# The last two units in front of five norms finish token tile 0 first, with one weight part held back

## The chip, the cores and the metric

One core of a Trainium2 chip runs one program. The metric is the device time of an execution in microseconds, lower is better. The engines are PE (TensorE), ACT (ScalarE), DVE (VectorE), POOL (GpSimd) and SP (SyncE, which issues the loads). Each runs its own list of instructions in order, and they wait for each other through semaphores that are written out by hand.

## What is computed

Three transformer layers on 256 tokens of width 1024, all in float32. The parts around which the change lies, cut from the reference:

```python
def rms_norm_2(x, g):
    x32 = x.astype(jnp.float32)
    y = x32 * lax.rsqrt(jnp.mean(x32 * x32, axis=-1, keepdims=True) + EPS)
    return (y * g.astype(jnp.float32)).astype(x.dtype)

def ada_modulation(c, ada_w, ada_b):
    m = jax.nn.silu(c) @ ada_w + ada_b
    return jnp.split(m, N_MOD, axis=-1)

def even_layer(x, c, ...):
    sh_m, sc_m, g_m, sh_f, sc_f, g_f = ada_modulation(c, ada_w, ada_b)
    h = modulate(rms_norm_2(x, mix_norm), sh_m, sc_m)
    ...                                   # h @ w_in, convolutions, LRU
    x = x + g_m[:, None, :] * y           # y = ... @ w_out
    hf = modulate(rms_norm_2(x, ffn_norm), sh_f, sc_f)
    return x + g_f[:, None, :] * swiglu(hf, ffn_w_gate, ffn_w_up, ffn_w_down)
```

First comes a layer of attention and a squared-ReLU MLP with norms before and after each branch, then `even_layer`, then `odd_layer` (the same with attention in place of convolutions and LRU).

## The kernel before, in words

**Tokens.** The 256 tokens are two tiles of 128 partitions, tile 0 and tile 1. The residual `x` and the normed `xn` lie tokens by features. For the next product they are transposed by PE (`norm_T`, L1864: two groups of four 128x128 blocks for each tile) and copied out of PSUM as `aT_hi` (ACT, rounded, L753) and `aT_lo` (DVE, the rest, L1132).

**Weights.** All weights are streamed once. A unit is 2048 columns, two parts of 128x1024. A part is loaded into `w_raw`, rounded by ACT into `w_hi` (`split_part`, L700), and the rest is formed by DVE in `w_lo` (L1124). Each product is hi times hi, hi times lo and lo times hi. There are four slots, part v uses slot v modulo 4, and ACT's split of part v waits until PE has used part v-4 (`w_used`). The load of part v waits until DVE has formed the rest of part v-4.

**Norms.** Six places normalise `x`, numbered k = 0 to 5: before the first QKV, the MLP, w_in, the first SwiGLU, the second QKV and the second SwiGLU. Before each of k = 1 to 5 PE ends a projection into the four banks of `acc` (`acc[:, 2t+c]` is column half c of tile t). The last units are `out_unit` with `tile0=True` for k = 1, 3, 5 (the last unit runs tile 0 first, then signals `tile0_done`), and `down(..., final=True)` for k = 2 and 4. DVE adds the result to `x`, ACT squares and sums it, the reciprocal root comes from ACT or POOL, DVE scales (`norm_rows`, L1147), PE transposes, ACT and DVE copy, and `entry` starts the next product (L1909) with tile 0, transposing tile 1 in between.

**Order on ACT at k = 3, 4, 5** (`norm`): for t in 0, 1 it waits for `x_ready` of tile t and squares the whole row (L710). The copies `norm_hi(k, 0)` of tile 0's transposes stand behind both squares at k = 3 and 5, and between them at k = 4:

```python
for t in range(NT):
    act.wait_ge(x_ready, 2 * (k - 1) + t + 1)
    row_square(t, x[:, t, :])
    ...
    if t == 0 and k == 4:
        norm_hi(k, 0)
if k in (3, 5):
    norm_hi(k, 0)
```

**Modulation sums.** `mod` holds partial sums of the modulation over partitions. `ada_sums` multiplies it by a matrix of ones (L2089, float32, two instructions for a chunk of 512 columns), which sums over the partitions and spreads the result; ACT copies it back (`ada_parts`, L764). Three or four of these sums stand in front of the transposes of k = 1, 2, 3, 4, 5; at k = 1 and 2 a fourth stands in front of tile 1's transposes.

Of the kernel before, what the change touches and what calls it, by code (L numbers as in the profile page):

```python
# [32 lines left out]
P = 128  # L33
# [82 lines left out]
def block_program(nc, a, out):  # L116
    ctx = ExitStack()
    with ctx:
# [125 lines left out]
        def sum_bank(m):  # L244

            if m < 8:
                return (tp[:, 1, :] if m < 4 else acc[:, 1, :], ub[:, 0, :], ub[:, 1, :], acc[:, 2, :])[m % 4]
            return (tp if m < 12 else ub)[:, m % 2, :]

        def flat(h):  # L250
            return h.rearrange("p b n -> p (b n)")

# [36 lines left out]
        half_done = sem("half_done")  # L289
        tile0_done = sem("tile0_done")  # L290
        mix_loaded = [sem(f"mix_loaded{n}") for n in range(6)]
# [390 lines left out]
        def _(act):  # L682
# [13 lines left out]
            def split_part(v, i=None, per=0):  # L696
                act.wait_ge(w_loaded[v % SLOTS], plus(16 * (v // SLOTS + 1), i, 16 * 2 * per // SLOTS))
                if v >= SLOTS:
                    act.wait_ge(w_used, plus(v - SLOTS + 1, i, 2 * per))
                act.activation(w_hi[:, v % SLOTS, :], w_raw[:, v % SLOTS, :], ACT.Copy).then_inc(hi_done, 1)  # L700
# [143 lines left out]
            def mlp_norm(u):  # L844

                n_norm[0] += 1
                act.wait_ge(w_used, parts_to(u - 1))
                half_square(0, 0, acc[:, 0, :], sq_half)
                half_square(1, 0, acc[:, 2, :], sq_half)
# [3 lines left out]
                split_part(2 * u + 2)  # L853
# [8 lines left out]
                norm_hi(1, 0)  # L862
                split_part(2 * u + 3)
# [50 lines left out]
            def win_norm(u):  # L914
# [12 lines left out]
                split_part(2 * u + 2)  # L927
# [5 lines left out]
                norm_hi(2, 0)  # L933
                split_part(2 * u + 3)
# [172 lines left out]
        def _(dve):  # L1107
# [13 lines left out]
            def split_part(v, i=None, per=0):  # L1121
                dve.wait_ge(hi_done, hi_count(v, i, per))
                n = v % SLOTS
                dve.tensor_tensor(w_lo[:, n, :], w_raw[:, n, :], w_hi[:, n, :].bitcast(F32),  # L1124
# [15 lines left out]
            def norm_rows(t, g, shift):  # L1140
# [4 lines left out]
                for g in range(2):  # L1145
                    c = slice(g * CH, (g + 1) * CH)
# [581 lines left out]
            gated_norm_halves(4, U_SG1, GATE_M, G_F, SH_F, 22)  # L1728
# [6 lines left out]
        def _(pe):  # L1735
# [3 lines left out]
            def project_tile(v, t, k, outp, op_hi, op_lo, start, stop):  # L1739

                s, q = v % SLOTS, slice(t * P, (t + 1) * P)
                for n in range(2):
                    c = slice(n * CH, (n + 1) * CH)
                    pe.matmul(outp, op_hi[:, k + n, q], w_hi[:, s, c], start=start and n == 0, stop=False)  # L1744
                    pe.matmul(outp, op_hi[:, k + n, q], w_lo[:, s, c], start=False, stop=False)  # L1745
                    last = pe.matmul(outp, op_lo[:, k + n, q], w_hi[:, s, c], start=False, stop=stop and n == 1)  # L1746
                return last

            def project(u, h, bank, i=None, per=0, first=0, operand=None, tile0=False, lo_count=0, parts=(0, 1)):

                op_hi, op_lo = operand or (aT_hi[:, 4 * h:4 * h + 4, :], aT_lo[:, 4 * h:4 * h + 4, :])
                if lo_count:
                    for q in range(2):
                        part_ready(2 * u + q, i, per)
                        for t in range(NT):
                            for k in range(2 * q, 2 * q + 2):
                                c = slice((k % 2) * CH, (k % 2 + 1) * CH)  # L1760
                                for w in (w_hi, w_lo):
                                    pe.matmul(bank(t), op_hi[:, k, t * P:(t + 1) * P], w[:, (2 * u + q) % SLOTS, c],
                                              start=h == first and k == 0 and w is w_hi, stop=False)
                    pe.wait_ge(y_lo, lo_count)
                    for q in range(2):
                        for t in range(NT):
                            for k in range(2 * q, 2 * q + 2):
                                c = slice((k % 2) * CH, (k % 2 + 1) * CH)
                                last = pe.matmul(bank(t), op_lo[:, k, t * P:(t + 1) * P], w_hi[:, (2 * u + q) % SLOTS, c],
# [518 lines left out]
```

## Time and profile before

| | |
|---|---|
| three executions | 901.29, 901.52, 902.69 us, median 901.52 |
| profiled execution | 901.51 us, of which the span of instructions is 899.4 us |
| PE busy | 888.7 us, 99% of the span |
| DVE, ACT, POOL busy | 695.0, 487.3, 29.3 us |
| granted TensorE clock | 1.00 of full speed |

How to read it: time is microseconds from the first instruction. Matmuls are pipelined, so the time that a matmul adds is the distance from its start to the next one's, and a wait of PE is where this distance is longer than usual. "Idle before" in square brackets is shorter than such a wait, because the end of a matmul lies behind the start of the next one.

### The profile page before, as it was taken

Reading aid. Unit: us, or ns where it says so; the run is one execution under the profiler, and the core shown is the slowest. Engines: PE = TensorE matmul, PEld = TensorE weight load, DVE = VectorE, ACT = ScalarE, POOL = GpSimd, SP = SyncE. Lnnn points to the kernel's source line nnn. Section 1 sums busy time; section 2 is a strip of 40 time slices with the busy share of each in tenths; the row PEclk is TensorE's granted clock in tenths of the full one; section 3 lists DMA queues with packets and bytes.
Section 4 is the critical chain, followed back from the end, with each engine's and each line's share of the span. In section 5 each row is a group of like instructions: output and inputs, shape, how many; then the busy total and the mean of one; then the engine's idle time right before and its main releaser. Section 6 shows DMA issues by size and latency. Waiting matters only on the chain.

```text
span 899.4 us, 13652 instructions
## 1 busy us (share of the span) xinstructions
PE 888.7 (99%) x5057; PEld 761.6 (85%) x5057; DVE 695.0 (77%) x723; ACT 487.3 (54%) x651; POOL 29.3 (3%) x52
## 2 busy tenths in 40 slices
PE   8999999999999999999999999999999999999998
PEld 5998879999999699979888888878777888888886
DVE  5698978988888887996888888687796775655655
ACT  5545574444445758755455455455675465545542
POOL 4000100000000000011000000010000100000000
PEclk9999999999999999999999999999999999999999
DMA  6989586999898385556988887636434365555561
GB/s 217 341 276 340 175 293 208 365 358 320 333 326 316 102 277 170 181 165 201 360 304 318 318 297 280 189 98 211 137 115 142 117 209 190 187 187 186 187 188 69
DMA packets 117093, 208.08 MB, mean 231 GB/s; under 512 B 7236, under 2 KB 81068, under 8 KB 111928
## 3 DMA queue, kind: packets, MB, share of 16 engines
q1 hardware_dynamic: 116566, 205.31, 66.8%
q10 hardware_dynamic: 290, 2.10, 0.7%
q8 instruction: 30, 0.49, 0.2%
q14 instruction: 15, 0.12, 0.0%
q0 software_dynamic: 192, 0.05, 0.0%
HBM read 206.39 MB, written 1.05 MB: 231 GB/s over the span
## 4 chain that ended last, share of the span: by engine, by line
PE 94%; ACT 2%; DVE 2%; DMA 1%; issue 0%; SPq 0%; DVEq 0%; ACTq 0%
PE tp L1891 8%; PE ub L1891 8%; PE acc L1796 7%; PE acc L1797 7%; PE acc L1799 7%; PE acc L1744 5%; PE acc L1746 5%; PE acc L1745 5%; PE tp L1892 4%; PE ub L1892 4%; PE tp L1909 4%; PE acc L1909 4%; PE ub L1880 3%; PE ub L1879 3%; PE ub L1878 3%; PE acc L1878 3%
## 5 line engine op out<-in xcount | busy, mean ns | idle before, releaser
L1124 DVE TENSOR_TENSOR w_lo<-w_raw,w_hi 128x1024 fp32r<-128x1024 f32 x288 | 348.7, 1221 | 115.1 <-ACT w_hi L700 114.4
L700 ACT ACTIVATE w_hi<-w_raw 128x1024 fp32r<-128x1024 f32 x288 | 302.3, 1058 | 241.8 <-PE acc L1799 71.0
L1891 PE MATMUL tp<-aT,w_hi 128*128 128x512 f32 x320 | 114.1, 399 | 0.0
L1891 PE MATMUL ub<-aT,w_hi 128*128 128x512 f32 x320 | 113.8, 398 | 0.0
L1796 PE MATMUL acc<-w_hi,hT_hi 128*128 128x512 f32 x288 | 112.8, 392 | 0.1
L1797 PE MATMUL acc<-w_lo,hT_hi 128*128 128x512 f32 x288 | 112.2, 390 | 0.0
L1799 PE MATMUL acc<-w_hi,hT_lo 128*128 128x512 f32 x272 | 106.1, 390 | 0.0
L1892 PE MATMUL tp<-aT,w_lo 128*128 128x256 f32 x320 | 89.9, 281 | 0.0
L1892 PE MATMUL ub<-aT,w_lo 128*128 128x256 f32 x320 | 89.8, 281 | 0.0
L1891 PEld LDWEIGHTS tp<-aT,w_hi 128*128 128x128 f32 x320 | 60.1, 188 | 14.9
L1891 PEld LDWEIGHTS ub<-aT,w_hi 128*128 128x128 f32 x320 | 60.1, 188 | 14.6
L1878 PE MATMUL ub<-aT,w_hi 128*128 128x256 f32 x256 | 72.5, 283 | 0.0
L1880 PE MATMUL ub<-aT,w_lo 128*128 128x256 f32 x256 | 72.4, 283 | 0.0
L1879 PE MATMUL ub<-aT,w_hi 128*128 128x256 f32 x256 | 72.4, 283 | 0.0
L1744 PE MATMUL acc<-w_hi,aT 128*128 128x512 f32 x168 | 67.5, 402 | 0.2 <-DVE aT L1132 0.2
L1746 PE MATMUL acc<-w_hi,aT 128*128 128x512 f32 x168 | 65.5, 390 | 0.0
L1745 PE MATMUL acc<-w_lo,aT 128*128 128x512 f32 x168 | 65.5, 390 | 0.0
L1796 PEld LDWEIGHTS acc<-w_hi,hT_hi 128*128 128x128 f32 x288 | 54.1, 188 | 11.6 <-issue 0.3
L1797 PEld LDWEIGHTS acc<-w_lo,hT_hi 128*128 128x128 f32 x288 | 54.1, 188 | 10.5
L1892 PEld LDWEIGHTS ub<-aT,w_lo 128*128 128x128 f32 x320 | 60.4, 189 | 0.7
L1799 PEld LDWEIGHTS acc<-w_hi,hT_lo 128*128 128x128 f32 x272 | 51.1, 188 | 11.3
L1892 PEld LDWEIGHTS tp<-aT,w_lo 128*128 128x128 f32 x320 | 60.4, 189 | 0.0
(282 smaller groups left out, 1526.8 us busy)
## 6 DMA issues: line engine op xcount, KB each, us to landing
ada_raw<-in_l_ada_w SPq DMA_DIRECT2D x24, 1024.0 KB, 6.0
w_raw<-in_l_ffn_w_gate SPq DMA_DIRECT2D x44, 512.0 KB, 4.6
w_raw<-in_l_ffn_w_up SPq DMA_DIRECT2D x44, 512.0 KB, 3.8
w_raw<-in_l_ffn_w_down SPq DMA_DIRECT2D x44, 512.0 KB, 3.4
w_raw<-in_w_up SPq DMA_DIRECT2D x32, 512.0 KB, 4.5
w_raw<-in_w_down SPq DMA_DIRECT2D x32, 512.0 KB, 5.2
scratch<-in_l_ada_w SPq DMA_DIRECT2D x14, 1024.0 KB, 7.7
w_raw<-in_attn_w_qkv SPq DMA_DIRECT2D x24, 512.0 KB, 6.3
```

Source lines behind the costliest of these rows:

```text
L700: act.activation(w_hi[:, v % SLOTS, :], w_raw[:, v % SLOTS, :], ACT.Copy).then_inc(hi_done, 1)
L1124: dve.tensor_tensor(w_lo[:, n, :], w_raw[:, n, :], w_hi[:, n, :].bitcast(F32), ALU.subtract).then_inc(lo_done, 1)
L1744: pe.matmul(outp, op_hi[:, k + n, q], w_hi[:, s, c], start=start and n == 0, stop=False)
L1745: pe.matmul(outp, op_hi[:, k + n, q], w_lo[:, s, c], start=False, stop=False)
L1746: last = pe.matmul(outp, op_lo[:, k + n, q], w_hi[:, s, c], start=False, stop=stop and n == 1)
L1796: pe.matmul(outp, operand[0][:, k, q], w_hi[:, s, c], start=start, stop=False)
L1797: last = pe.matmul(outp, operand[0][:, k, q], w_lo[:, s, c], start=False, stop=False)
L1799: last = pe.matmul(outp, operand[1][:, k, q], w_hi[:, s, c], start=False, stop=stop)
L1878: pe.matmul(outp, wh, aT_hi[:, b, :], start=b == 0, stop=False)
L1879: pe.matmul(outp, wh, aT_lo[:, b, :], start=False, stop=False)
L1891: pe.matmul(banks[f], w_hi[:, v % SLOTS, c], aT[:, :, b, :], start=b == 0, stop=False)
L1892: last = pe.matmul(banks[f][:, 0:TOK], w_lo[:, v % SLOTS, c], aT_hi[:, b, :], start=False, stop=b == KB - 1)
```

## The change

The diff does five things.

- Before k = 1, 3 and 5 a new `out_last` takes the place of the last two units. With four parts v to v+3 it runs tile 0 with v, tile 1 with v, tile 0 with v+1 (signal `tile0_first`), tile 0 with v+2 and v+3 (signal `tile0_done`), and then tile 1 with v+1, v+2, v+3. Before k = 2 and 4 `down(..., left=...)` does the like: tile 1 with the second part of the last unit but one is run after `tile0_done`.
- Since part v+1 is held longer, a part four further on is put into a buffer that is idle then (`apart`), and the odd slots of the last layer change places (`slot_of`), so that the splits don't wait for the held part.
- Two sums stand before tile 0's transposes, the third directly behind them (`behind_T0`), the fourth before tile 1's transposes (`before_T1`), at all five places.
- DVE takes tile 0 whole first, then the first half of tile 1, then `norm_rows(0)`, and then the second half of tile 1. ACT's order is changed in `mlp_norm` and `win_norm` alone.
- `norm_rows` can wait for its shift by halves.

```diff
@@ ACT, mlp_norm
-                act.wait_ge(w_used, parts_to(u - 1))
+                act.wait_ge(tile0_first, 1)
                 half_square(0, 0, acc[:, 0, :], sq_half)
-                half_square(1, 0, acc[:, 2, :], sq_half)
                 act.wait_ge(tile0_done, 1)
                 half_square(0, 1, acc[:, 1, :], sq_done)
                 half_rstd(0, 1, 1)
-                split_part(2 * u + 2)
+                act.wait_ge(w_used, parts_to(u - 1))
+                half_square(1, 0, acc[:, 2, :], sq_half)
...
                 norm_hi(1, 0)
+                split_part(2 * u + 2)
                 split_part(2 * u + 3)
@@ ACT, win_norm
                 half_rstd(0, 1, 6)
-                split_part(2 * u + 2)
...
                 norm_hi(2, 0)
+                split_part(2 * u + 2)
                 split_part(2 * u + 3)
@@ DVE
             def gated_norm(n, u_end, g_mod, g, shift):
 
+                dve.wait_ge(half_done, n)
+                gated(0, g_mod, 0)
                 dve.wait_ge(tile0_done, n + 1)
-                gated(0, g_mod).then_inc(x_ready, 1)
+                gated(0, g_mod, 1).then_inc(x_ready, 1)
                 dve.wait_ge(x_ready, 2 * n + 1)
                 norm_scale(0, g)
+                dve.wait_ge(half_done, n + 1)
+                dve.tensor_tensor(xn[:, 1, 0:CH], acc[:, 2, :], g_mod[:, 0:CH], ALU.mult).then_inc(tile1_gated, 1)
+                norm_rows(0, g, shift)
                 dve.wait_ge(w_used, parts_to(u_end))
-                gate(1, g_mod)
-                norm_rows(0, g, shift)
+                gate(1, g_mod, 1)
+                dve.wait_ge(tile1_gated, 1)
                 add_gated(1).then_inc(x_ready, 1)
...
             def gated_norm_halves(n, u_end, g_mod, g, shift, out):
 
                 split_part(2 * u_end)
-                dve.wait_ge(w_used, parts_to(u_end - 1))
-                for t in range(NT):
-                    gated(t, g_mod, 0)
+                dve.wait_ge(tile0_first, n // 2 + 1)
+                gated(0, g_mod, 0)
+                if out:
+                    split_part(2 * u_end + 1)
                 dve.wait_ge(tile0_done, n + 1)
                 gated(0, g_mod, 1).then_inc(x_ready, 1)
                 dve.wait_ge(x_ready, 2 * n + 1)
                 norm_scale(0, g)
+                dve.wait_ge(w_used, parts_to(u_end - 1))
+                gated(1, g_mod, 0)
+                norm_rows(0, g, shift, out)
+                if not out:
+                    split_part(2 * u_end + 1)
                 dve.wait_ge(w_used, parts_to(u_end))
                 gated(1, g_mod, 1).then_inc(x_ready, 1)
-                if out:
-                    dve.wait_ge(ada_out, out)
-                norm_rows(0, g, shift)
-                split_part(2 * u_end + 1)
                 dve.wait_ge(x_ready, 2 * n + 2)
                 norm_scale(1, g)
@@ PE, entry
                 norm_T(k, 0)
+                behind_T0()
...
@@ PE, new
+            def out_last(u, order, lo_count=0):
+                v, h = 2 * u + 4, order[2][1]
...
+                else:
+                    part_ready(v)
+                    tile(0, 0)
+                    tile(1, 0).then_inc(w_used, 1)
+                    part_ready(v + 1)
+                    tile(0, 1).then_inc(tile0_first, 1)
+                for p in (2, 3):
+                    part_ready(v + p)
+                    last = tile(0, p)
+                last.then_inc(tile0_done, 1)
+                for p in (1, 2, 3):
+                    tile(1, p).then_inc(w_used, 1)
@@ PE, down, final
                     lo(0, 1, 1).then_inc(tile0_done, 1)
+                    if left:
+                        for n in range(2):
+                            last = down_block(2 * u - 1, left[0], 1, n, False, False, operand=operand)
+                        last.then_inc(w_used, 1)
@@ PE, before the entries
-            ada_sums(0, 0, 3)
-            entry(U_MLP, tp_banks, before_T1=lambda: ada_sums(0, 3, 4), tile1_out=1)
+            ada_sums(0, 0, 2)
+            entry(U_MLP, tp_banks, lambda: ada_sums(0, 2, 3), lambda: ada_sums(0, 3, 4), tile1_out=1)
...
-            ada_sums(1, 0, 4)
             def swiglu(layer):
...
-                entry(u, tp_banks, gated=True)
+                m = 8 * layer
+                ada_sums(1, m, m + 2)
+                entry(u, tp_banks, lambda: ada_sums(1, m + 2, m + 3), lambda: ada_sums(1, m + 3, m + 4), gated=True)
```

## Rows read from the trace of the kernel before

**Rows 1.** The page, part 1: busy us, share of the span, instructions.
```profile
PE 888.7 (99%) x5057; PEld 761.6 (85%) x5057; DVE 695.0 (77%) x723; ACT 487.3 (54%) x651; POOL 29.3 (3%) x52
```

**Rows 2.** Waits of PE: waiting line, releaser: us in total, times, longest.
```profile
PE acc L1909 <- ACT aT L753: 1.7, 3, 0.9
```

**Rows 3.** Timeline of PE at k = 3: start us, us, instruction, count.
```profile
389.07 0.39 PE L1744 MATMUL acc<-w_hi,aT 128*128 128x512 f32 x1
...
394.51 3.98 PE L2089 MATMUL ub<-ada_raw,ones 128*128 128x512 f32 x8
...
399.62 0.74 PE L1909 MATMUL tp<-w_hi,aT 128*128 128x256 f32 x4
...
403.71 1.03 PE L1864 MATMUL acc<-ident,xn 128*128 128x128 f32 x8
```

**Rows 4.** Timeline of DVE at k = 3.
```profile
389.58 1.23 DVE L1124 TENSOR_TENSOR w_lo<-w_raw,w_hi 128x1024 fp32r<-128x1024 f32 x1 [1.10 <-ACT w_hi L700]
390.73 0.68 DVE L1243 TENSOR_TENSOR xn<-acc,mod 128x512 f32<-128x512 f32 x1
...
392.05 0.68 DVE L1243 TENSOR_TENSOR xn<-acc,mod 128x512 f32<-128x512 f32 x1
...
396.81 0.69 DVE L1247 TENSOR_TENSOR x<-x,xn 128x512 f32<-128x512 f32 x1
397.42 1.41 DVE L1147 SCALAR_TENSOR_TENSOR xn<-xn,rstd,mod 128x512 f32<-128x512 f32 x2
```

**Rows 5.** Timeline of ACT at k = 3.
```profile
388.42 2.01 ACT L700 ACTIVATE w_hi<-w_raw 128x1024 fp32r<-128x1024 f32 x2 [3.47 <-PE acc L1769]
...
397.53 1.06 ACT L710 ACTIVATE scratch<-x 128x1024 f32<-128x1024 f32 x1 [0.50 <-DVE x L1247]
...
398.97 1.20 ACT L753 ACTIVATE aT<-acc 128x512 fp32r<-128x512 f32 x2 [0.28 <-PE acc L1864]
```

**Rows 6.** Timeline of PE at k = 5.
```profile
704.14 3.70 PE L2089 MATMUL ub<-mod,ones 128*128 128x512 f32 x8
...
708.96 0.74 PE L1909 MATMUL tp<-w_hi,aT 128*128 128x256 f32 x4
...
713.00 1.04 PE L1864 MATMUL acc<-ident,xn 128*128 128x128 f32 x8
```

**Rows 7.** Timeline of ACT at k = 5: the copy of the second sum.
```profile
706.06 0.60 ACT L764 ACTIVATE mod<-ub 128x512 f32<-128x512 f32 x1 [0.26 <-PE ub L2089]
```

**Rows 8.** Timeline of PE at k = 2.
```profile
302.38 1.02 PE L2089 MATMUL acc<-mod,ones 128*128 128x512 f32 x2
...
305.31 1.32 PE L1864 MATMUL tp<-ident,xn 128*128 128x128 f32 x8 [0.20 <-DVE xn L1147]
307.57 1.19 PE L1909 MATMUL acc<-w_hi,aT 128*128 128x512 f32 x4 [0.94 <-ACT aT L753]
```

**Rows 9.** Timeline of DVE at k = 2.
```profile
298.29 1.23 DVE L1124 TENSOR_TENSOR w_lo<-w_raw,w_hi 128x1024 fp32r<-128x1024 f32 x1 [0.36 <-ACT w_hi L700]
...
304.52 1.40 DVE L1147 SCALAR_TENSOR_TENSOR xn<-xn,rstd,mod 128x512 f32<-128x512 f32 x2
```

**Rows 10.** Timeline of PE at k = 4.
```profile
586.03 1.88 PE L2089 MATMUL ub<-mod,ones 128*128 128x512 f32 x4
...
591.83 1.18 PE L1909 MATMUL acc<-w_hi,aT 128*128 128x512 f32 x4 [0.25 <-ACT aT L753]
...
595.86 1.03 PE L1864 MATMUL ub<-ident,xn 128*128 128x128 f32 x8
```

**Rows 11.** Timeline of DVE at k = 4.
```profile
586.09 1.23 DVE L1138 TENSOR_TENSOR xn<-x,mod 128x1024 f32<-128x1024 f32 x1
...
588.61 1.41 DVE L1147 SCALAR_TENSOR_TENSOR xn<-xn,rstd,mod 128x512 f32<-128x512 f32 x2
```

**Rows 12.** Timeline of PE at k = 1.
```profile
120.41 1.18 PE L1909 MATMUL tp<-w_hi,aT 128*128 128x512 f32 x4
```

**Rows 13.** Timeline of PE at k = 0, the first products of the program.
```profile
9.24 2.07 PE L1909 MATMUL acc<-w_hi,aT 128*128 128x512 f32 x4 [0.49 <-ACT aT L753]
```

More of the change, by code:

```diff
@@ L1760, in project @@
                                 c = slice((k % 2) * CH, (k % 2 + 1) * CH)
-                                for w in (w_hi, w_lo):
-                                    pe.matmul(bank(t), op_hi[:, k, t * P:(t + 1) * P], w[:, (2 * u + q) % SLOTS, c],
-                                              start=h == first and k == 0 and w is w_hi, stop=False)
+                                for w in (rounded_part, rest_part):
+                                    pe.matmul(bank(t), op_hi[:, k, t * P:(t + 1) * P], w(2 * u + q)[:, c],
+                                              start=h == first and k == 0 and w is rounded_part, stop=False)
                     pe.wait_ge(y_lo, lo_count)
@@ L1847, in down @@
                                 last = pe.matmul(acc[:, 2 * t + n, :], hT_lo[:, 2 * h, t * P:(t + 1) * P],
-                                                 w_hi[:, v % SLOTS, n * CH:(n + 1) * CH], start=False, stop=False)
+                                                 rounded_part(v)[:, n * CH:(n + 1) * CH], start=False, stop=False)
                     else:
-                        for t in range(NT):
+                        for t in range(1 if left and k == 1 else NT):
                             for n in range(2):
                                 last = down_block(v, 2 * h + k, t, n, first and k == 0, False, operand=operand)
-                    last.then_inc(w_used, 1)
+                    if not (left and k == 1):
+                        last.then_inc(w_used, 1)
             n_norm = [0]
@@ L1908, in products @@
                         width = HALF if gated else CH
-                        last = pe.matmul(out, op[:, b, t * P:(t + 1) * P], w[:, v % SLOTS, n * width:(n + 1) * width],
+                        last = pe.matmul(out, op[:, b, t * P:(t + 1) * P], part[:, n * width:(n + 1) * width],
                                          start=begin and n == 0, stop=end and n == blocks - 1)
@@ L1924, in entry @@
                         half(t, p)
-                        if t == 0 and w is w_hi:
+                        if t == 0 and w is hi:
                             pe.wait_ge(hi_done, hi_count(2 * u + p))
@@ L1928, in entry @@
                             part_ready(2 * u + p)
-                        products(t, p, aT_hi, w, p == 0 and w is w_hi)
+                        products(t, p, aT_hi, w, p == 0 and w is hi)
                     if t == 0:
@@ L1942, in entry @@
                         for p in range(2):
-                            products(1, p, aT_lo, w_hi).then_inc(w_used, 1)
+                            products(1, p, aT_lo, rounded_part).then_inc(w_used, 1)
                     else:
@@ L1950, in entry, with no_sums @@
                     part_ready(2 * u + p)
-                    products(0, p, aT_hi, w_lo, end=p == 3)
-                    products(1, p, aT_hi, w_lo)
-                    products(1, p, aT_lo, w_hi, end=p == 3).then_inc(w_used, 1)
+                    products(0, p, aT_hi, rest_part, end=p == 3)
+                    products(1, p, aT_hi, rest_part)
+                    products(1, p, aT_lo, rounded_part, end=p == 3).then_inc(w_used, 1)
+            def no_sums():
+                return None
             def hidden_T(h, out):
@@ L2085, in ada_sums @@
                     c, m = ADA_ORDER[layer][n], 12 * layer + n
-                    if m >= 8:
+                    if m >= 8 and m not in (18, 19):
                         pe.wait_ge(ada_out, m - 1)
@@ L2184, in one @@
                     pe.wait_ge(hT_lo_done, plus(j0 + j, i, 2))
-                    down(v + 2, (j - 1) % 2, i, 6, first=j == 1)
+                    down(v + 2, (j - 1) % 2, i, 6, first=j == 1, left=last_left if i is None and j == NJ_SG - 1 else ())
                 one(1)
```

160 lines of the change are left out of this document (102 added, 58 removed).

## Prediction

> **What bounds the kernel now.** The page first: PE is busy 99% of the span [rows 1], so the time is PE's work plus its waits, and the change adds or removes no matmul, load or copy. What it can win or lose is PE's waits at five places. The waits of PE come next: the products behind the norms wait 1.7 us for ACT's copies of the transposes, three times [rows 2]. Then the timeline around each norm, where the distance from one start to the next is set against the usual one. The usual ones: 24 matmuls from 389.07 to 394.51 are 0.2267 each [rows 3]; a sum is two instructions of 0.43, so 0.86 (four take 1.88, of which the last's own length is 0.60) [rows 10]; eight transposes are 8 x 0.109 = 0.87; a product of the SwiGLU entry (256 columns) is 0.12. By these, PE loses about 0.8 us at k = 1, 1.9 at k = 2, 1.1 at k = 3, 1.9 at k = 4 and 0.7 at k = 5: 6.4 us in all are there to be won.
>
> The method for each place is the same. The first sum begins where the units end, and that doesn't move, since the units keep their matmuls. From there I put down PE's own list (two sums, transposes, sum, products, sum, transposes of tile 1) and see whether what it needs from ACT and DVE is later. The result is how far the transposes of tile 1 move, because behind them nothing waits before or after. A release comes 0.4 us after the start of the last matmul of a group, since one lasts 0.39 [rows 3].
>
> **k = 2 (w_in): gain 1.35.** Tile 0 is done 6 matmuls, 1.36 us, sooner. ACT's split of the second w_in part doesn't wait for the held part, so DVE's rest of it starts behind the instruction before at 297.85 and not at 298.29, where it stood 0.36 for ACT [rows 9]; the scaling of tile 0's second half, which waited for tile 0's end, follows at 299.6 and not 300.6. All behind it shifts by 1.0: `norm_rows(0)` from 304.52 to 303.5 [rows 9]. PE ends two sums at 302.38 + 1.72 = 304.1 [rows 8] and transposes at 304.3, not 305.31 [rows 8]. ACT's split of 1.06 that stood in front of tile 1's squares goes behind the copies, so these come at 305.0. The third sum covers them: 304.3 + 0.2 + 0.87 + 0.86 gives the first product at 306.3, not 307.57 [rows 8]. With the 0.1 that a product costs behind a wait, the gain is 1.35. The moved splits end at 308.1, and PE asks for the later one at 306.3 + 10 x 0.2267 = 308.5: cover of 0.4.
>
> **k = 4 (second QKV): gain 1.6.** Counted back from the first sum at 586.03 [rows 10], tile 0's first half is released 25 matmuls before it, at 586.03 - 5.67 + 0.4 = 580.8, and all of tile 0 at 586.03 - 19 x 0.2267 + 0.4 = 582.1. ACT's second split doesn't wait for the held part and ends at 580.1, DVE's rest behind it at 581.6. Two halves of 1.32 [rows 4] end at 584.2; before, tile 0 was whole just ahead of 586.09, and `norm_rows(0)`, at 588.61, began 2.5 behind it [rows 11]. Of these 2.5, 2.1 are the square and POOL's root and the rest is a gate of tile 1 that stood in the way; so it begins at 586.5 at the latest, if the root is alone. PE has ended two sums at 586.03 + 1.72 = 587.75 [rows 10], transposes at once, and sums until 589.5; ACT's copies begin at 588.4 and hide behind the third. First product 589.5 and not 591.83 [rows 10]: 2.3 sooner, of which 0.86 is the fourth sum, only moved; 0.1 is won at the first product. Tile 1's transposes then come at 594.2, not 595.86 [rows 10].
>
> **k = 1 (MLP): gain 0.1.** `norm_rows(0)` comes 0.7 sooner, but PE stood only 0.1 us for it. Two sums, the transposes and the third sum end at 120.36, and the first product began at 120.41 before [rows 12]; the list is the same and only a stand of 0.1 goes. For tile 1 ACT now has two splits (1.06 + 0.96) between the copies and the squares and not one, which eats the 0.7: tile 1 is normed between 0.1 sooner and 0.2 later. I take 0.1 sooner.
>
> **k = 3 (first SwiGLU): loss 1.8.** Here the order on ACT is unchanged: the copies of tile 0's transposes stand behind the square of tile 1's row, which waits for `x_ready` of tile 1. The change puts `norm_rows(0)` and a split of DVE in front of that `x_ready`. DVE's list: ACT's split is released 4 matmuls sooner (388.42 less 0.91) [rows 5], so DVE's rest begins at 388.6 and gives place after 1.15 [rows 4]. Two halves of tile 0 at 1.32 each (390.73 to 392.05) end at 392.5; `norm_scale` takes 1.26 (its 1.23 and the wait for its own end) [rows 11]; a half of tile 1 1.32; `norm_rows` 1.33 (1.41, but each instruction gives place 0.08 before its end, as 389.58 to 390.73 shows for one of 1.23); the split 1.14; the last half of tile 1 1.41, to its end [rows 4]. That ends at 399.0. Before it was 396.81 + 0.69 = 397.50 [rows 4]. ACT squares from 399.0, gives place after 1.04, copies for 0.6 (two take 1.20) [rows 5]: first product 400.7, not 399.62 [rows 3]. PE has done two sums, transposes and the third sum by 394.51 + 1.72 + 0.87 + 0.86 = 398.0 and stands for 2.7 us. From the first product to tile 1's transposes it was 4.09 (399.62 to 403.71) [rows 3], of which 0.2 were small waits that go; the fourth sum comes in: 400.7 + 3.9 + 0.86 = 405.5, which is 1.8 later than 403.71.
>
> **k = 5 (second SwiGLU): loss 2.3.** The same order. DVE is early, but `norm_rows(0)` of the second half waits for the second sum's copy, which starts at 706.06 and takes 0.60 [rows 7], and PE's sums don't come sooner. So it runs 706.7 to 707.4, the last half of tile 1 ends 1.41 later at 708.8, the square gives place at 709.85, and the first product comes at 710.5, not 708.96 [rows 6]. PE's third sum ends at 708.8: a stand of 1.7 us, beside 0.85 and 0.4 before the two groups of transposes. Then 3.9 + 0.86: tile 1's transposes at 715.3 and not 713.00 [rows 6].
>
> **Sum.** -0.1 - 1.35 + 1.8 - 1.6 + 2.3 = +1.05 us. The buffers `apart` cost nothing: they are written by the same split, and the loads of the parts concerned have landed before. What the trace doesn't show is a change of weights from transposes to a sum and on to a product without a wait between: between 0 and 0.1 us at each of five places; I take 0, by the matmul behind another kind, and 0.5 for the range. Against the profiled execution, 901.51, which is the median, this gives 902.6.
>
> **A clock that falls.** The first products of the program take 2.07 for four [rows 13], where four take 1.18 at k = 1 [rows 12]: a start distance of 0.43 and not 0.23, PE's lower of two levels, though the page's granted clock says 1.00. After that no matmul of the trace is so slow, and the longest stand is 1.1 us, at k = 2 (305.31 + 0.87 + 0.3 of waits within, to 307.57) [rows 8]. The change makes one of 2.7. The Trainium skill ("TensorE: Matmul & The Clock Gate", What's actually happening) says that the array falls to half its rate after a stretch of idleness and comes back after a stretch of work; the trace agrees at the program's start, and no row shows it for a stand of 2 to 3 us.
>
> **Rivals.**
> - *The two SwiGLU norms don't stall (faster).* If the copies of tile 0 don't end up behind the later square, or DVE's list is 2 us shorter than my sum, k = 3 gives -1.1 and k = 5 +0.5 (its `norm_rows` still waits for the sum's copy). Then it is -0.1 - 1.35 - 1.1 - 1.6 + 0.5 = -3.6: 897.9. For it: DVE's work at k = 3 does begin 1 us sooner. Against it: the order on ACT as it stands in the code. If only one of the two stalls goes, 899.7 to 900.
> - *The clock falls in a stand (slower).* It decides at the stand of 2.7 us at k = 3, or at those of k = 5. At the start PE is slow from 6.8 to 12.4; as much at half the rate costs 2.8 us. One fall gives 905.4, two 908.
> - *The change doesn't do what it says*: `tile0_first` or the held part brings nothing at k = 2 and 4, because another wait (a load, a split) ends last. Then it is +4.0: 905.5. Against it: the loads for these parts have landed more than 1 us before.
>
> **How the numbers follow.** The forecast 902.6 has a chance of 0.68 and its own range 901.7 to 903.8 (0.3 for each DVE list, 0.5 for the changes of weights). The faster rival with its in-between cases has 0.17, the clock 0.09, no gain at k = 2 and 4 0.06. For 8 in 10 the range is 898.8 to 904.8. A measurement can tell about 0.2%, 1.8 us, from no change. Above 903.3 lie the two slower rivals and a fifth of the forecast, 0.28; below 899.7 most of the faster rival, 0.15; between them 0.57.
>
> **What would show it.** Right: at k = 3 a wait of L1909 for ACT's aT of over 2 us with the square of tile 1 (L710) just before the copy; at k = 5 one of some 1.6; at k = 2 the product at 306.3 and at k = 4 at 589.5; start distances of 0.227 behind the stands. Wrong: the copy (L753) at k = 3 in front of the second square, `x_ready` of tile 1 before 398, distances of 0.43 behind a stand, or waits of PE for `w_hi` or `w_lo` inside the entries.

## The result, and the profile after

The changed kernel takes 904.29 us (median of 9 executions, 902.78 to 906.05), the kernel before 901.59 us (9 executions, 901.29 to 902.69). The ratio is 1.0025, with a 95% interval of 1.0017 to 1.0034. The forecast of 902.6 and its range (898.8 to 904.8) hold that median, but the direction doesn't agree with the likeliest case: 2.7 us more is slower by over 0.2%, which had a chance of 0.28. The range holds it by 0.5 us, and the same kernel's second median below (904.81) lies on its edge.

The nine executions are of two kinds. In four (902.78, 902.97, 903.02, 903.23) TensorE's mean granted clock is 0.999 or 1.0, and their mean is 903.0. In five (904.29, 904.63, 905.10, 905.23, 906.05) it is 0.998, and their mean is 905.1. The profiled one is 903.23, of the first kind, with a span of 901.1. The page has PE busy 99% of it, as in [rows 1]. A stand is a stretch in which PE does nothing and waits. Its length is given here as the profile counts idle time, which is 0.16 us less than the distance of starts makes it at k = 3 and 5. The waits of PE (engine, tile and line, what was waited for: us in total, times, the longest), against [rows 2]:

```profile
PE tp L1934 <- ACT aT L779: 4.1, 2, 2.6
PE acc L2052 <- DMA gain<-in_norm_mix_pre: 2.7, 1, 2.7
PE acc L1888 <- DVE xn L1175: 0.7, 1, 0.7
```

In the new line numbers L1934 are the products, L1888 the transposes, L2158 the sums, L779 ACT's copies of the transposes, L736 the square of a row, L1175 the normed rows. The two waits that make 4.1 us are new: they stand in front of the first products of the two SwiGLU norms, k = 3 and k = 5. The first wait of the program (gain) is 2.7 where the trace of before has 2.3, and in the traces below between 2.3 and 3.1: it lies ahead of all that was changed, and it moves everything behind it. So 0.4 of the 1.7 us between the two profiled executions is no effect of the change.

The timeline of PE at k = 3 (start, duration, engine, line, operation, tiles, count, idle time before and what ended it), which answers to [rows 3]:

```profile
393.58 1.88 PE L2158 MATMUL ub<-ada_raw,ones 128*128 128x512 f32 x4
395.30 1.07 PE L1888 MATMUL acc<-ident,xn 128*128 128x128 f32 x8
396.21 1.02 PE L2158 MATMUL ub<-ada_raw,ones 128*128 128x512 f32 x2
399.84 0.74 PE L1934 MATMUL tp<-w_hi,aT 128*128 128x256 f32 x4 [2.61 <-ACT aT L779]
...
401.86 2.11 PE L1934 MATMUL tp<-w_hi,aT 128*128 128x256 f32 x16
403.81 1.02 PE L2158 MATMUL ub<-ada_raw,ones 128*128 128x512 f32 x2
404.67 1.04 PE L1888 MATMUL acc<-ident,xn 128*128 128x128 f32 x8
405.46 0.72 PE L1934 MATMUL tp<-w_hi,aT 128*128 128x256 f32 x4
```

The transposes follow the first two sums at once, 1.72 us behind the start of the first one where it was 3.82 before, and with the third sum done PE stands 2.6 us. The same stretch of DVE and of ACT shows why:

```profile
394.25 1.41 DVE L1175 SCALAR_TENSOR_TENSOR xn<-xn,rstd,mod 128x512 f32<-128x512 f32 x2
395.57 1.22 DVE L1150 TENSOR_TENSOR w_lo<-w_raw,w_hi 128x1024 fp32r<-128x1024 f32 x1
...
397.43 0.69 DVE L1275 TENSOR_TENSOR x<-x,xn 128x512 f32<-128x512 f32 x1
```

```profile
398.16 1.06 ACT L736 ACTIVATE scratch<-x 128x1024 f32<-128x1024 f32 x1 [2.06 <-DVE x L1275]
...
399.21 1.07 ACT L779 ACTIVATE aT<-acc 128x512 fp32r<-128x512 f32 x2
```

ACT is idle for 2.06 us with the finished transposes in front of it: its next instruction in order is the square of tile 1's row, which waits for DVE's last sum of `x`, and the copies (L779) stand behind it. At k = 5 it is the same picture, [rows 6] before and this after:

```profile
703.53 1.88 PE L2158 MATMUL ub<-mod,ones 128*128 128x512 f32 x4
706.10 1.44 PE L1888 MATMUL acc<-ident,xn 128*128 128x128 f32 x8 [0.69 <-DVE xn L1175]
...
709.88 0.74 PE L1934 MATMUL tp<-w_hi,aT 128*128 128x256 f32 x4 [1.48 <-ACT aT L779]
...
714.71 1.04 PE L1888 MATMUL acc<-ident,xn 128*128 128x128 f32 x8
```

At k = 2 and k = 4 the stands are gone ([rows 8] and [rows 10] before):

```profile
304.62 1.32 PE L1888 MATMUL tp<-ident,xn 128*128 128x128 f32 x8
...
306.24 1.49 PE L1934 MATMUL acc<-w_hi,aT 128*128 128x512 f32 x4
...
312.24 0.93 PE L1934 MATMUL acc<-w_hi,aT 128*128 128x512 f32 x3
```

```profile
588.71 1.04 PE L1888 MATMUL tp<-ident,xn 128*128 128x128 f32 x8
...
590.05 1.47 PE L1934 MATMUL acc<-w_hi,aT 128*128 128x512 f32 x4
...
596.03 1.17 PE L1934 MATMUL acc<-w_hi,aT 128*128 128x512 f32 x4
```

**The account.** One mark for each place, the start of the first product behind the transposes of tile 1, gives what each did. In the trace of before these are the lines

```profile
126.01 1.17 PE L1909 MATMUL tp<-w_hi,aT 128*128 128x512 f32 x4
...
313.16 1.17 PE L1909 MATMUL acc<-w_hi,aT 128*128 128x512 f32 x4
...
404.50 1.67 PE L1909 MATMUL tp<-w_hi,aT 128*128 128x256 f32 x12
...
596.65 1.17 PE L1909 MATMUL acc<-w_hi,aT 128*128 128x512 f32 x4
...
713.79 1.67 PE L1909 MATMUL tp<-w_hi,aT 128*128 128x256 f32 x12
```

and in that of after, beside the last lines of the views above at k = 2, 3 and 4,

```profile
126.32 0.93 PE L1934 MATMUL tp<-w_hi,aT 128*128 128x512 f32 x3
...
715.50 0.72 PE L1934 MATMUL tp<-w_hi,aT 128*128 128x256 f32 x4
```

Before and after: 126.01 and 126.32 at k = 1, 313.16 and 312.24 at k = 2, 404.50 and 405.46 at k = 3, 596.65 and 596.03 at k = 4, 713.79 and 715.50 at k = 5. The lead or lag (after less before) goes +0.31, -0.92, +0.96, -0.62, +1.71, and the steps of it, with the 0.43 of the program's start (the first sum of k = 1 comes at 116.85 and not 116.42) taken from the first, are -0.12, -1.23, +1.88, -1.58, +2.33. Their sum is +1.28, and 0.43 + 1.28 = 1.71 is the difference of the two profiled executions (1.72). What is left of the 2.7 us of the medians is not in this trace: it is in the executions that show the lower mean clock.

### The profile page after: what moved, and what is told of

The parts are those of the page before. It is cut to its first block, busy times and chain, and to the rows that moved or that the text cites. A ratio compares the mean times of both kernels' runs of the same rounds, so it can differ in the third digit from the quotient of the medians.

```text
span 901.1 us, 13655 instructions
## 1 busy us (share of the span) xinstructions
PE 887.9 (99%) x5057; PEld 761.9 (85%) x5057; DVE 694.9 (77%) x726; ACT 487.3 (54%) x651; POOL 28.9 (3%) x52
## 3 DMA queue, kind: packets, MB, share of 16 engines
HBM read 206.39 MB, written 1.05 MB: 230 GB/s over the span
## 4 chain that ended last, share of the span: by engine, by line
PE 95%; DVE 3%; ACT 1%; DMA 1%; issue 1%; SPq 0%; ACTq 0%; DVEq 0%
PE tp L1915 8%; PE ub L1915 8%; PE acc L1816 7%; PE acc L1817 7%; PE acc L1819 7%; PE acc L1779 5%; PE acc L1781 5%; PE acc L1780 5%; PE tp L1916 4%; PE ub L1916 4%; PE acc L1934 4%; PE tp L1934 4%; PE ub L1904 3%; PE ub L1903 3%; PE ub L1902 3%; PE acc L1902 3%
## 5 line engine op out<-in xcount | busy, mean ns | idle before, releaser
L1150 DVE TENSOR_TENSOR w_lo<-w_raw,w_hi 128x1024 fp32r<-128x1024 f32 x283 | 342.6, 1222 | 110.4 <-ACT w_hi L726 110.0
L726 ACT ACTIVATE w_hi<-w_raw 128x1024 fp32r<-128x1024 f32 x283 | 296.6, 1058 | 232.8 <-PE acc L1819 67.4
L1779 PE MATMUL acc<-w_hi,aT 128*128 128x512 f32 x160 | 64.4, 402 | 0.2 <-DVE aT L1158 0.2
L1781 PE MATMUL acc<-w_hi,aT 128*128 128x512 f32 x160 | 62.4, 390 | 0.0
L1780 PE MATMUL acc<-w_lo,aT 128*128 128x512 f32 x160 | 62.4, 390 | 0.0
```

The lines of the kernel that those rows point to most:

```text
L726: act.activation(rounded_part(v), w_raw[:, v % SLOTS, :], ACT.Copy).then_inc(hi_done, 1)
L1150: dve.tensor_tensor(rest_part(v), w_raw[:, v % SLOTS, :], rounded_part(v).bitcast(F32), ALU.subtract).then_inc(lo_done, 1)
L1779: pe.matmul(outp, op_hi[:, k + n, q], wh[:, c], start=start and n == 0, stop=False)
L1780: pe.matmul(outp, op_hi[:, k + n, q], wl[:, c], start=False, stop=False)
L1781: last = pe.matmul(outp, op_lo[:, k + n, q], wh[:, c], start=False, stop=stop and n == 1)
```

## The experiments

The theory behind all of them: PE's time goes by its own ordered list and by the two ordered lists of ACT and DVE. The loss at k = 3 and 5 is made by ACT's order (copies behind a square that waits for a later `x`), the gain at k = 2 and 4 is real, and the rest of the slowdown is TensorE's clock falling behind the stand at k = 3. The kernel before was timed beside each group: 901.49 for the first four, 901.58 for the next four, 902.09 for the last two, on another chip each time.

**1. The changed kernel once more.** No edit.

> The changed kernel itself, unaltered, as the measure for the others. Its nine executions so far lie in two groups: four of 902.8 to 903.2 us with a granted clock of 0.999 to 1.000, five of 904.3 to 906.1 with 0.998. Theory A (the stands of PE at k = 3 and k = 5 sometimes let the clock fall): again two groups, about half of the executions 1.3 to 3 us above the lowest and with the lower clock. Rival B (the spread was that chip's or that hour's): one group within 0.5 us near 903.

904.81 us (903.03 to 905.38, 7 executions), ratio 1.0031 [1.0020, 1.0042]. One execution has a clock of 1.0 (903.03), six have 0.997 or 0.998 (904.33 to 905.38, mean 904.8). Here the profiled execution is of the second kind (904.87), so the fall can be seen. The timeline of PE at k = 3:

```profile
400.03 0.75 PE L1934 MATMUL tp<-w_hi,aT 128*128 128x256 f32 x4 [2.61 <-ACT aT L779]
400.62 0.99 PE L1934 MATMUL tp<-w_lo,aT 128*128 128x256 f32 x4
401.40 1.05 PE L1934 MATMUL tp<-w_hi,aT 128*128 128x256 f32 x4
402.26 1.05 PE L1934 MATMUL tp<-w_lo,aT 128*128 128x256 f32 x4
403.11 2.50 PE L1934 MATMUL tp<-w_hi,aT 128*128 128x256 f32 x16
```

Between the starts of groups of four lie 0.78, 0.86 and 0.85 us, so 0.213 for each product of the last two groups, where the trace above has 0.12 (16 products from 401.86 to 403.81). The table of stretches gives the granted clock for it (stretch, its length, busy time and count of PE, PEld, DVE, ACT, POOL, then the clock, the DMA share and GB/s):

```profile
400.00:405.00 5.00, 4.97 (x29) 4.97 (x30) 3.75 (x5) 2.84 (x4) 2.37 (x3) 0.66 0.05 16
405.00:420.00 15.00, 15.00 (x109) 13.81 (x108) 7.83 (x8) 7.37 (x9) 2.76 (x3) 1.00 0.49 146
```

The clock is 0.66 in the 5 us behind the stand and 1.00 in the other stretches of the table: for about 3.6 us PE runs at its lower level, 1.2 GHz. Some 17 products at 0.094 us more each cost 1.6 us. Behind the stand of k = 5, which is 1.5 us, nothing of the kind is seen (1.00 from 710 to 716).

**2. Both copies first.** In ACT's norm, at k = 3 and 5, the copies of tile 0 and the splits of the next weights go in front of the square of tile 1; nothing else of the change is touched.

```diff
-                    if t == 0 and k == 4:
+                    if t == 0 and k in (4, 3, 5):
                         norm_hi(k, 0)
+                        if k != 4:
+                            split_hi(u + 1)
                 if k in (3, 5):
-                    norm_hi(k, 0)
-                if k in (3, 5):
-                    split_hi(u + 1)
                     ada_parts(layer, parts[2], parts[3])
```

> The changed kernel, but at k = 3 and 5 ACT copies tile 0's transposes and makes the two splits before it squares tile 1's row. Theory (the square of tile 1 in front of the copies is what makes PE stand): the stand of 2.77 at k = 3 and that of 1.64 before the first product at k = 5 go; tile 1's transposes come 2.3 sooner at k = 3 (then limited by tile 1's norm) and 1.5 at k = 5; span 897.2, time 899.3, 0.25% under the kernel before. Rival (the copies wait for something else, such as tile 0's norm or PE): no more than 0.5 us changes. On the clock: by theory A all executions show 1.000 and lie within 0.5 us; by rival B the spread stays.

898.93 us (898.57 to 899.29, 6), ratio 0.9969 [0.9957, 0.9981], no execution with a lower clock: 4.1 us less than the changed kernel's executions whose clock holds, and 5.4 less than its median. The timeline of PE and of ACT at k = 3:

```profile
396.25 1.02 PE L2157 MATMUL ub<-ada_raw,ones 128*128 128x512 f32 x2
396.71 1.04 PE L1933 MATMUL tp<-w_hi,aT 128*128 128x256 f32 x4
```

```profile
396.04 1.08 ACT L778 ACTIVATE aT<-acc 128x512 fp32r<-128x512 f32 x2
...
398.89 1.07 ACT L736 ACTIVATE scratch<-x 128x1024 f32<-128x1024 f32 x1
```

The copies start at 396.04 and not 399.21, the products at 396.71 and not 399.84, right behind the sum. (The product is recorded 0.46 us behind the start of a sum that takes 0.86, so the distance of 3.1 us says too much: tile 1's transposes come at 402.23 and not 404.67, 2.4 us sooner.) The square of tile 1 comes 0.7 later than it did, and PE doesn't ask for it. So the copies' place in ACT's list is what makes the stand.

**3 and 4. One of the two places alone.** The same edit at k = 3 only, and at k = 5 only (`k in (4, 3)`, `k in (4, 5)`).

> The same order of ACT at k = 3 alone, so the stand of 1.64 at k = 5 (and 0.85 before the transposes there) stays. Theory: span 898.8, time 900.9. Clock: if only a stand as long as the 2.77 at k = 3 lets it fall, none falls here; if the 1.64 at k = 5 is enough, some executions lie 1.3 to 3 us higher with 0.998.

> The same order of ACT at k = 5 alone, so the stand of 2.77 at k = 3 stays. Theory: span 899.6, time 901.6 in the executions whose clock holds. Clock: if the stand at k = 3 is the cause, about half of the executions fall to 0.998 and lie 1.3 to 3 us higher; if it is the one at k = 5, none.

At k = 3 alone: 900.79 us (900.09 to 901.58, 11), ratio 0.9989 [0.9980, 0.9998], no lower clock in 11 executions, although the stand of k = 5 is still there. At k = 5 alone: 902.86 us (901.18 to 903.58, 11), ratio 1.0011 [1.0002, 1.0020]; eight of 11 show a clock of 0.997 or 0.998 (mean 903.1), three hold it (901.18, 901.33, 901.83, mean 901.4). In its trace the stretch behind the stand of k = 3 has again a clock of 0.66:

```profile
400.00:405.00 5.00, 4.84 (x28) 4.84 (x29) 3.75 (x5) 2.97 (x5) 2.37 (x3) 0.66 0.07 23
```

Against the 903.0 of the changed kernel with its clock held, mending k = 3 gives 2.2, mending k = 5 gives 1.6, and both give 4.1. The lower clock belongs to the stand at k = 3 and goes with it.

**5. The kernel before with a stand made by hand.** Does the stand itself lower the clock, or something else that the change brought? The kernel before gets three squares more on ACT at k = 3, in front of its copies, chained one behind the other (two of a whole row, one of half a row; nobody reads them).

```diff
+                if k == 3:
+                    act.wait_ge(sq_done, n_sq[0])
+                    for width in 2 * (D,) + 1 * (CH,):
+                        chained(act.activation(squares[:, 1, 0:width], x[:, 1, 0:width], ACT.Square))
                 if k in (3, 5):
                     norm_hi(k, 0)
```

> The kernel before, with nothing of the change, but at k = 3 ACT squares tile 1's row again, twice whole and once by half, each waiting for the one ahead, in front of the copies of tile 0's transposes (nobody reads these squares; the output is unaffected). PE then stands about 3.0 us behind the transposes where it stood 0.3. Theory (a stand of this length is by itself enough to let the clock fall): 904.1 in the executions whose clock holds, and in half of them or more a clock of 0.998 and 1.6 more, 905.7. Rival (the fall needs something else of the change, such as the four sums and their order before the stand, or is this program's loads): all executions at 904.1 with 1.000.

904.98 us (903.88 to 906.20, 6), ratio 1.0036 [1.0024, 1.0049]. Three executions hold the clock (903.88, 903.94, 904.66), three don't (905.30, 905.34, 906.20). The kernel before, timed beside it, has no lower clock in 17. The trace is of one that holds it:

```profile
402.86 0.74 PE L1913 MATMUL tp<-w_hi,aT 128*128 128x256 f32 x4 [2.67 <-ACT aT L757]
403.44 0.64 PE L1913 MATMUL tp<-w_lo,aT 128*128 128x256 f32 x4
```

So the stand alone, in a kernel without any of the change, is enough, and the fall isn't certain. That the length differs from one execution to the next doesn't explain it: the two traces of the changed kernel both have a stand of 2.61 at k = 3, and the clock holds in the first and falls in the second. A fall costs 1.5 us here (means 904.2 and 905.6).

**6. A shorter stand.** In the changed kernel, at k = 3 alone, the fourth sum comes directly behind the third, so PE has 0.86 us more work before the stand, which is 1.75 us then and not 2.61. All else, ACT's order too, is as changed.

```diff
-                entry(u, tp_banks, lambda: ada_sums(1, m + 2, m + 3), lambda: ada_sums(1, m + 3, m + 4), gated=True)
+                if layer:
+                    entry(u, tp_banks, lambda: ada_sums(1, m + 2, m + 3), lambda: ada_sums(1, m + 3, m + 4), gated=True)
+                else:
+                    entry(u, tp_banks, lambda: ada_sums(1, m + 2, m + 4), no_sums, gated=True)
```

> The changed kernel with one sum moved: at k = 3 the fourth sum stands behind the third, behind tile 0's transposes, and no longer before tile 1's. It fills 0.86 of the stand, which falls from 2.77 to 1.9; the copies don't come sooner. Theory (the loss at k = 3 is the stand of 1.0 beyond before plus the sum that was moved behind it): 0.86 less than the changed kernel where the clock holds, 902.2. Rival (PE's place is set by tile 1's norm and not by its own list): no gain. On the clock: 1.6 let none of eleven executions fall, 2.77 let nine of eleven; if the length decides, few or none fall at 1.9 and the median is 902.3, 2.5 under the changed kernel's.

902.08 us (901.66 to 903.71, 11), ratio 1.0008 [0.9999, 1.0017], no lower clock in 11 executions.

```profile
395.91 1.88 PE L2158 MATMUL ub<-ada_raw,ones 128*128 128x512 f32 x4
399.55 0.75 PE L1934 MATMUL tp<-w_hi,aT 128*128 128x256 f32 x4 [1.75 <-ACT aT L779]
```

(The expectation counts stands by distance, 2.77 and 1.9, and its nine falls of eleven are eight in the record of `copies_first_k5`.) The sum is now hidden in the stand, which is worth its 0.86, and the fall is gone: 903.0 - 0.9 = 902.1. This separates the two parts of the loss.

**7. Only k = 2 and 4.** The change with k = 1, 3 and 5 put back to what they were before (units, order of ACT and DVE, sums). The two places with `down(..., left=...)`, for which the gain was forecast, stay. Of the edit, the two cuts on PE that take back the units and the sums at k = 5 and at k = 3 and 5:

```diff
-                    if n < 28:
-                        out_unit(U_WOUT1, OUT_LO_FIRST, n // 2 - 12, (hT_hi, hT_lo), parts=(n % 2,))
-                    elif n == 28:
-                        out_last(U_WOUT1, OUT_LO_FIRST)
+                    if n != 31:
+                        out_unit(U_WOUT1, OUT_LO_FIRST, n // 2 - 12, (hT_hi, hT_lo) if n < 28 else None,
+                                 parts=(n % 2,))
...
-                ada_sums(1, m, m + 2)
-                entry(u, tp_banks, lambda: ada_sums(1, m + 2, m + 3), lambda: ada_sums(1, m + 3, m + 4), gated=True)
+                ada_sums(1, m, m + 4)
+                entry(u, tp_banks, no_sums, no_sums, gated=True)
```

> The change at k = 2 and 4 alone: held part, order of ACT and DVE and places of the sums there; k = 1, 3 and 5 as in the kernel before. Theory (the places are independent and each is worth what its stretch of the trace shows, 1.23 and 1.58 us): 901.5 - 2.8 = 898.7. Rival (a gain at one place is given back at the next, since splits, loads or tile 1's chain fall behind): more than 900.

898.83 us (898.51 to 899.53, 6), ratio 0.9968 [0.9955, 0.9980]: 2.75 us less than before, where the account above has 1.23 + 1.58 = 2.81. The rival that nothing is gained at k = 2 and 4 falls. It is also as fast as `copies_first`: with ACT's order mended, the new scheme at k = 3 and 5 brings nothing on balance. By the same marks as above, `copies_first` gains 0.6 at k = 3 and loses 0.8 at k = 5, where the transposes wait for the rows that are normed from the second sum's copy.

**8. The sums of k = 5 sooner.** `copies_first`, and at k = 5 the first two sums between the end of tile 0 and tile 1's parts, so that their copies are there in time; ACT's splits on either side of its square.

```diff
-def out_last(u, order, lo_count=0):
+def out_last(u, order, lo_count=0, between=None):
...
                 last.then_inc(tile0_done, 1)
+                if between:
+                    between()
...
-                        out_last(U_WOUT1, OUT_LO_FIRST)
+                        out_last(U_WOUT1, OUT_LO_FIRST, between=lambda: ada_sums(1, 8, 10))
```

> The kernel with the copies in front of the square at k = 3 and 5, and at k = 5 also the first two sums between the end of tile 0 and tile 1's parts in the last units, with one split behind the square. Theory (at k = 5 tile 0's norm waits for the copy of the second sum, which starts 1.9 us behind the end of the units): the 0.85 and 0.30 in front of the two groups of transposes go, tile 1's transposes then wait for their own norm, in all 1.0 less: 897.9. Rival (DVE's additions to x are what ends last there): no gain, 898.9.

898.26 us (898.17 to 899.61, 5), ratio 0.9966 [0.9952, 0.9979], where 897.9 was expected. The two waits in front of the groups of transposes at k = 5 went, and a new one came in the products, for the second split:

```profile
707.48 1.66 PE L1937 MATMUL tp<-w_hi,aT 128*128 128x256 f32 x12 [0.47 <-ACT w_hi L726]
```

**9. The same with both splits in front of the square.** 

```diff
                         if k == 5:
-                            split_part(2 * u + 2)
-                if k == 5:
-                    split_part(2 * u + 3)
+                            split_hi(u + 1)
```

> sums_early with one line moved: at k = 5 both splits of ACT stand in front of the square of tile 1, and not one on either side. In sums_early the second split was waited for by PE (0.63 us at 706.7), while the normed tile 1 was ready 1.6 us before PE asked for it, so the square may come 1.0 us later. Theory (PE's own list with the waits of ACT and DVE on it): the 0.63 goes, about 0.1 of it turns up elsewhere, 898.26 - 0.55 = 897.7, and no execution with a lower clock. Rival (tile 1's norm is what ends last at k = 5): the transposes of tile 1 wait for the later square and it stays at 898.3 or rises to 898.7.

898.16 us (897.47 to 898.73, 5) beside 902.09 for the kernel before on that chip, ratio 0.9952 [0.9939, 0.9966]. The wait for the split is gone, and the transposes of tile 1 begin without one and take 0.2 us longer (1.01 us from their start to the next product, 0.79 in `sums_early`):

```profile
706.88 2.08 PE L1935 MATMUL tp<-w_hi,aT 128*128 128x256 f32 x16
708.80 1.02 PE L2161 MATMUL ub<-mod,ones 128*128 128x512 f32 x2
709.66 1.26 PE L1889 MATMUL acc<-ident,xn 128*128 128x128 f32 x8
```

So the rival (tile 1's norm ends last) isn't what the trace shows, beyond those 0.2. The time alone doesn't decide it: 898.16 as measured lies beside the rival's 898.3, while on 901.5 the ratio is 897.2, near the 897.7 expected. Its interval and that of `sums_early` overlap, so what lies between the two is seen in the traces and not in the times. Of all kernels here this one stands lowest against the kernel before.

**10. DVE's order put back.** The loss has two halves in the code: ACT's copies stand behind the square, and DVE now norms tile 0 ahead of the last half of tile 1, which makes the square late. Experiment 2 takes away the first. This one takes away the second and leaves ACT as it is.

```diff
                 gated(1, g_mod, 0)
-                norm_rows(0, g, shift, out)
                 if not out:
                     split_part(2 * u_end + 1)
                 dve.wait_ge(w_used, parts_to(u_end))
                 gated(1, g_mod, 1).then_inc(x_ready, 1)
+                norm_rows(0, g, shift, out)
```

> The changed kernel, with only DVE's order of before restored at k = 3 and 5: the last half of tile 1's gate and sum stands in front of the normed rows of tile 0, and ACT's order stays. x_ready of tile 1 then comes at 396.8 and not 398.16, and ACT's copies don't come late behind its square, but tile 0's normed rows end at 398.2 and not 395.6. Theory (the loss is made by ACT's order alone, and DVE can only move the wait from the copies to the transposes): at k = 3 the transposes start at 398.2, the third sum ends and the first product starts at 399.9, as now (399.84), with the stand in two pieces, 2.0 in front of the transposes; at k = 5 transposes at 707.3 and product at 709.05, not 709.88, so 0.8 is won. Sum: 903.0 - 0.8 = 902.2, and since no piece is as long as 2.8, no execution with a lower clock. Rival (DVE's new order is what costs, so that taking it back returns the loss of 1.9 and 2.3): 899 to 900.

903.42 us (900.73 to 904.50, 11) beside 902.09, ratio 1.0006 [0.9997, 1.0016]. Four executions hold the clock (900.73 to 901.90, mean 901.5), seven don't (mean 903.8). Neither line of the expectation holds whole. That no execution would fall was wrong, and the gain is larger than the 0.8 written down: with the clock held the kernel is 0.6 below its own before, where the changed kernel is 1.5 above, so 2.1 us are won. The trace (of an execution that fell):

```profile
394.41 1.88 PE L2158 MATMUL ub<-ada_raw,ones 128*128 128x512 f32 x4
399.10 1.82 PE L1888 MATMUL acc<-ident,xn 128*128 128x128 f32 x8 [2.81 <-DVE xn L1175]
400.71 1.92 PE L2158 MATMUL ub<-ada_raw,ones 128*128 128x512 f32 x2
```

```profile
706.08 1.88 PE L2158 MATMUL ub<-mod,ones 128*128 128x512 f32 x4
709.11 1.32 PE L1888 MATMUL acc<-ident,xn 128*128 128x128 f32 x8 [1.15 <-DVE xn L1175]
...
710.72 1.03 PE L1934 MATMUL tp<-w_hi,aT 128*128 128x256 f32 x4
```

As the theory had it, the stand moves from the copies to the transposes. At k = 5 the first product comes 4.64 us behind the first sum and not 6.35, 1.7 sooner, not 0.8: the expectation let the transposes wait for both instructions of the normed rows, and they wait for the first only, 0.8 behind its start (708.31 to 709.11). At k = 3 the stand is 2.8 us and not 2.0. The 2.0 doesn't follow from the expectation's own times: transposes at 398.2, behind two sums that end at 395.3, leave 2.9. By its own rule (no piece as long as 2.8) a fall was to be expected, and falls came. That 2.8 was measured is two differences that cancel. The transposes wait for the first instruction only, some 0.7 sooner, and DVE's list is 0.8 later there: ACT's split waits for a load of w_gate that landed later in this execution (388.17, with an idle time of 3.33 for the DMA, against 386.58 and 2.56 in the trace of after; PE is 0.83 later, ACT 1.59). Behind the stand eight transposes take 1.61 us to the next start where the trace of after has 0.91, and the clock is low:

```profile
398.00:404.00 6.00, 4.90 (x23) 3.77 (x24) 5.95 (x9) 4.73 (x7) 2.14 (x3) 0.72 0.29 90
```

So neither engine's order alone makes the loss: mending either wins, 4.1 us with ACT's, about 2.1 with DVE's.

## Why the prediction came out as it did, step by step

**The terms of the sum were right.** Predicted and measured, from the account: 0.1 and 0.12 won at k = 1, 1.35 and 1.23 at k = 2, 1.8 and 1.88 lost at k = 3, 1.6 and 1.58 won at k = 4, 2.3 and 2.33 lost at k = 5. The sum was +1.05 and is +1.28. The working holds in detail as well, each number shifted by the lead or lag with which its place begins. At k = 3 (0.92 early) `x_ready` was to come at 399.0 - 0.9 = 398.1, and the last sum ends at 397.43 + 0.69 = 398.12. At k = 5 (0.62 early) the first product was put at 710.5 - 0.6 = 709.9 and came at 709.88, tile 1's transposes at 715.3 - 0.6 = 714.7 and came at 714.71. The waits look as announced: one of 2.6 for `aT` with the square just in front of the copy, one of 1.5 at k = 5. One agreement has no margin: ACT's split at k = 3 starts at 386.58, as forecast (387.51 less 0.92), but the trace of after names a load as its releaser and not PE, and where that load landed later (experiment 10) the split moved 0.8 us with it.

**The named rivals.** That the two SwiGLU norms don't stall is refuted by the trace: they do, and experiment 2 shows that the stall is ACT's order. Made so by hand, the kernel gives 898.9; the rival's 897.9 had k = 5 lose 0.5 and k = 3 gain 1.1, where 0.8 and 0.6 came. That k = 2 and 4 bring nothing is refuted by experiment 7.

**The step that failed is the clock.** The forecast said of a stand of 2 to 3 us that no row shows what it does to the clock, gave the fall 0.09, and priced it at 2.8 us, by the slow start of the program. Its sign of being wrong, start distances of twice the usual behind a stand, is in the trace of `after_again`. In the runs it happens in 11 of the 16 executions of the changed kernel, so it is what the median shows, and it costs 1.5 to 2.3 us by the means of the two kinds of execution of one kernel (905.1 and 903.0; 904.8 and 903.0; 903.1 and 901.4; 905.6 and 904.2; 903.8 and 901.5), 1.6 by the distances in the trace. With chance and price as measured the forecast would have been 902.6 + 1.6 = 904.2 and "slower" the likeliest direction. So that the median still lies within the range is in part luck, with 5 falls in 9 executions and a price below the one that was forecast. The step failed in a way that the text had prepared: the mechanism was named, with its place and its sign, and the only row that bore on its chance was the longest harmless stand, 1.1 us, which says nothing of one of 2.7. Where two levels of one resource differ by a factor of two and the trace has no row between harmless and harmful, an even chance would have been nearer.

The Trainium skill ("TensorE: Matmul & The Clock Gate", What's actually happening) has the array fall to half its rate after idleness and return after work. The traces agree in kind (0.213 and not 0.12 between products, then the old distance again); that the same stand brings it in some executions and not in others is from the runs.

**What stays open.** Whether executions that hold the clock do so because of where the stand falls in time, or for a cause outside the core, no run tells: the profile of an execution shows its clock, not why. Between 1.75 us (0 of 11) and 2.6 us (most) no kernel was run. One of the 56 executions of the kernel before timed with the experiments shows 0.998 too (904.28), without a trace.

## What to carry to other kernels

When a step of one tile is moved ahead of another tile's, follow it through the ordered list of every engine: here DVE and PE were reordered and ACT was not, and its copies stood 2 us behind a square that waited for the other tile. When a stand of the matmul engine grows by more than those that the trace shows as harmless, count a fall of its clock as a main case and not as a remote one. A sum or two of the matmul engine's other work put into the stand (0.86 us here) is then worth twice: once for itself, once for the clock.

## What the runs showed of the hardware

Behind a stand of TensorE of 2.6 to 2.8 us, with full work before and after it, the clock falls to 1.2 GHz in many executions of a kernel and not in all: 11 of 16 of the changed kernel, 8 of 11 with k = 5 mended, 3 of 6 of the kernel before with a stand added, 7 of 11 with DVE's order put back. Where the longest stand after the program's start is 1.75 us (0 of 11) or 1.5 us (0 of 11), it was not seen. Three traces have it at k = 3. In two of them the granted clock from 400 to 405 us is 0.66, in the third 0.72 from 398 to 404. In that of `after_again` the products are 0.213 us apart, and after about 3.6 us the old distance is back. In the mean clock of the whole execution that is 0.002 or 0.003, which is easily read past: the difference shows in the table of stretches and in the distances of starts, and in a spread of times within one kernel of 3.3 us (902.78 to 906.05) where the kernel before has 1.4.
